# First norm of a two-block transformer kernel: every squared chunk summed on TensorE, the first phase table moved ahead of it on VectorE, block positions transferred before the input

## The chip, the core and the metric

One core of a Trainium2 chip runs the whole program. Its engines are TensorE (PE, with its weight loads shown as PEld), VectorE (DVE), ScalarE (ACT), GpSimd (POOL) and SyncE (SP), which here only issues transfers. Each runs its own stream of instructions in order, and they wait for each other by semaphores. The metric is the device time of one execution in microseconds (us).

## The reference

Input `x` is 512 tokens of width 1024, fp32. A first block (norm, a projection that feeds an S5 state-space branch and stick-breaking attention, gates, a feed-forward part) is followed by a second block of two layers (gated linear attention, forgetting attention, each with a per-layer embedding). What matters here is the first norm and what stands right behind it:

```python
def rmsnorm(x, g):
    xf = x.astype(jnp.float32)
    y = xf * lax.rsqrt(jnp.mean(xf * xf, axis=-1, keepdims=True) + EPS)
    return (y * g.astype(jnp.float32)).astype(x.dtype)
...
        u = rmsnorm(h, norm_mix[l])
        proj = u @ w_in[l]
        u_ssm, q, k, v = jnp.split(proj, [D_SSM, D_SSM + D_ATTN, D_SSM + 2 * D_ATTN], axis=-1)
```

The S5 branch needs, for each state, powers of `exp(lam * dt)` at the positions of the blocks of 4 tokens. Their angle is the "phase": block position times turns per token, less the whole turns.

## The kernel before

**Layout.** `h` holds the input feature-major: 8 chunks (DC) of 128 features on the partitions, 512 tokens along the free dimension. The fp32 products are made as three products of fp32r halves (`three`, L526 to L533: high by high, high by low, low by high), so each operand is split into a high and a low part: ScalarE makes the high part by a rounding copy (L1222), VectorE the low part by a subtraction.

**Weights.** 105 units of 1 MB (`wstream`) go through two slots `wraw`. SyncE issues the first two at the start (L433) and each further one when the low part of the unit before in the slot is done (L444 to L449). ScalarE splits high (`split_hi`, L1224), VectorE low (`split_lo`, L1908).

**Transfers at the start**, all on SyncE's queue, in this order (L423 to L442): the S5 parameters, `ones`, the input in four parts (`x_in`), `vecs`, `ident`, two weight units, the S5 coefficient matrices `s5b` (semaphore `bc_in`), then `headones`, `samechunk`, `reset` and `blockpos`, five constants to be rounded, and `wa2`. These last ten count on `cst_sem` (N_CST is 10).

**The first norm.** ScalarE squares the chunks (L1829 to L1831) into `first_square(c)`. VectorE's `first_norm` (L1983) adds chunks 0 to 6 into `acc`. TensorE sums over the partitions: a product whose stationary operand is 128 tokens of a squared chunk and whose moving operand is one column of ones. `first_sums` (L586) does that for the last chunk, then for `acc`, four products each, into four columns of a PSUM bank. VectorE then computes the reciprocal root by shift and three Newton steps (`norm_rms`, `rsqrt`, L1926 to L1950), TensorE spreads it over the partitions (`norm_spread`, L617), and VectorE scales each chunk (L2011), ScalarE rounds it, VectorE makes its low part (L2001), and the first projection unit (`gemm(0, ...)`) takes chunk by chunk.

**Unread products.** `unread(n)` (L581) issues n 128x512 fp32 products of a tile of zeros into a bank that nobody reads. The order on TensorE is written out by hand:

```python
            pe.wait_ge(x_in[1], 16)
            unread(3)
            pe.wait_ge(first_in, 48)
            first_sums()
            unread(2)
            norm_spread(0)
            unread(3)
            gemm(0, 0, two(0), 256, uhi, ulo, True, u_wait(0), ready=0)
```

**The phase and what follows.** On VectorE `s5_prepare` (L2032) makes the turns per token and per the low part. Behind `first_norm`, the second weight unit's low part and four small vector steps stands `phase(0)` (L2102): seven steps over 128x512, each waiting for the one before. ScalarE's `table(0)` (L1325) makes sine and cosine of it. Then VectorE builds the input maps (`in_maps(0)`, L2070), the low parts of queries and keys, and enters the loop of four mixers, in which the order on VectorE is `out_maps`, `softplus`, `fail_lo`, `turn_in` (with the repeated map, L2152), `w_lo` and so on. `phase(i + 1)` for the later mixers is made inside mixer i.

Of the kernel before, what the change touches and what calls it, by code (L numbers as in the profile page):

```python
# [21 lines left out]
ALU = mybir.AluOpType  # L22
# [3 lines left out]
P = 128  # L26
T = 512
D = 1024
DC = D // P
TT = T // P  # L30
# [51 lines left out]
CST = {}  # L82
# [39 lines left out]
def build(nc, wstream, xT, pT, vecs_d, cst_d, s5p_d, wa2_d, outT):  # L122
    ctx = ExitStack()
    with ctx:
# [3 lines left out]
        def sem(name):  # L128
            return ctx.enter_context(nc.semaphore(name))
# [12 lines left out]
        ones = sb("ones", [P, P])  # L142
        headones = sb("headones", [P, P])
# [162 lines left out]
        N_CST = 10  # L306
# [22 lines left out]

        x_in = [sem(f"x_in{k}") for k in range(X_PARTS)]  # L330
        first_in, cst_sem, par_in, pe_sem = sem("vectors_in"), sem("consts_in"), sem("params_in"), sem("ple_in")
        bc_in = sem("bc_matrices_in")
        out_sem = sem("out_stored")
        landed = [sem("weights_landed0"), sem("weights_landed1")]
        hi_done, lo_done = sem("weights_hi_done"), sem("weights_lo_done")
# [67 lines left out]
        def first_square(c):  # L403

            return pp[:, c, :] if c < DC - 2 else sq[:, c % 2, :]
# [15 lines left out]
        @block.sync  # L421
        def _(sp):
            sp.dma_start(s5p[:, 0:3, :], s5p_d[:, 0:48].rearrange("p (a b) -> p a b", a=3)).then_inc(par_in, 16)  # L423
            a, b = CST["ones"]
            sp.dma_start(ones[:, :], cst_d[:, a:b]).then_inc(first_in, 16)
            for k in range(X_PARTS):
                c = slice(k * DC // X_PARTS, (k + 1) * DC // X_PARTS)
                sp.dma_start(h[:, c, :], xT[:, c, :]).then_inc(x_in[k], 16)
            sp.dma_start(vecs[:, :], vecs_d).then_inc(first_in, 16)
            a, b = CST["ident"]  # L430
            sp.dma_start(ident[:, :], cst_d[:, a:b]).then_inc(first_in, 16)
            for n in range(2):
                sp.dma_start(wraw[:, n, :], wstream[n]).then_inc(landed[n], 16)  # L433
            sp.dma_start(s5b[:, :, :], s5p_d[:, 48:].rearrange("p (a b) -> p a b", a=4)).then_inc(bc_in, 16)
            for name, dst in (("headones", headones), ("samechunk", samechunk), ("reset", reset),
                              ("blockpos", blockpos)):
                a, b = CST[name]
                sp.dma_start(dst[:, :], cst_d[:, a:b]).then_inc(cst_sem, 16)
            for k, name in enumerate(("ones", "keymask", "querymask", "tri", "negones")):
                a, b = CST[name]  # L440
                sp.dma_start(cst_in[:, k, :], cst_d[:, a:b]).then_inc(cst_sem, 16)
            sp.dma_start(wa2[:, :], wa2_d).then_inc(cst_sem, 16)  # L442

            with nc.sync.Fori(0, (NU - 3) // 2) as i:  # L444
                for n in range(2):
                    sp.wait_ge(lo_done, i * 2 + (n + 1))
                    sp.dma_start(wraw[:, n, :], wstream[i * 2 + (n + 2)]).then_inc(landed[n], 16)
            sp.wait_ge(lo_done, NU - 2)
            sp.dma_start(wraw[:, 0, :], wstream[NU - 1]).then_inc(landed[0], 16)  # L449
            for k in range(TT // 2):  # L450
                for half in range(2):
                    for t, evacuated in ((2 * k, out_even), (2 * k + 1, out_odd)):
                        sp.wait_ge(evacuated, 2 * k + half + 1)
                        sp.dma_start(outT[:, t, half * T:half * T + T], h[:, 2 * t + half, :]).then_inc(out_sem, 16)
            sp.wait_ge(out_sem, 16 * DC)
# [69 lines left out]
        def _(pe):  # L525
# [55 lines left out]
            def unread(n):  # L581

                for _ in range(n):
                    nc.tensor.matmul(ps[:, 0, :], M[:, 0, :], M[:, :, :].rearrange("p q c -> p (q c)"), start=True, stop=True)

            def first_sums():  # L586

                pe.wait_ge(sq_done, DC)
                for t in range(TT):
                    nc.tensor.matmul(ps[:, SS_BANK[0], t:t + 1], first_square(DC - 1)[:, t * P:(t + 1) * P], ones[:, 0:1],  # L590
                                     start=t == 0, stop=False, skip_group_check=True)
                pe.wait_ge(acc_done, DC - 1)
                for t in range(TT):
                    mm = nc.tensor.matmul(ps[:, SS_BANK[0], t:t + 1], acc[:, t * P:(t + 1) * P], ones[:, 0:1], start=False,
                                          stop=True, skip_group_check=True)
                mm.then_inc(ss_done, 1)

            def norm_sums(j):

# [17 lines left out]
            def norm_spread(j, k=0, bank=None):  # L617

                pe.wait_ge(rs_done, j + 1)
                for t in range(TT):  # L620
                    mm = nc.tensor.matmul(ps[:, SS_BANK[j] if bank is None else bank, t * P:(t + 1) * P],  # L621
                                          rstd[:, k, t:t + 1].to_broadcast([P, P]), ident[:, :], start=True, stop=True)
                mm.then_inc(bc_done, 1)
# [533 lines left out]

            pe.wait_ge(bias_ready, 1)
            pe.wait_ge(x_in[1], 16)
            unread(3)  # L1160
            pe.wait_ge(first_in, 48)
            first_sums()
            unread(2)
            norm_spread(0)
            unread(3)
            gemm(0, 0, two(0), 256, uhi, ulo, True, u_wait(0), ready=0)
# [50 lines left out]
        def _(act):  # L1217
# [619 lines left out]
                other = HEAD_ROWS[1 - hh]  # L1837
                own.do(copy(kl[other, hh, :], zero_b[other, :].to_broadcast([64, T])))
            norm(0)
            act.wait_ge(bc_in, 16)  # L1840
            own.do(copy(s5b[:, 3, :], s5b[:, 3, :], -1.0))
            act.wait_ge(cst_sem, 16 * N_CST)
            for k, dst in enumerate((onesr, keymaskr, querymaskr, trir, negonesr)):
                copy(dst[:, :], cst_in[:, k, :]).then_inc(consts_ready, 1)
            copy(identr[:, :], ident[:, :]).then_inc(consts_ready, 1)
# [58 lines left out]
        def _(dve):  # L1904
# [77 lines left out]

            def first_norm():  # L1983

                for c in range(1, DC - 1):
                    dve.wait_ge(sq_done, c + 1)
                    if c >= 2:
                        dve.wait_ge(acc_done, c - 1)
                    V.tensor_tensor(acc[:, :], first_square(0) if c == 1 else acc[:, :], first_square(c),
                                    ALU.add).then_inc(acc_done, 1 if c < DC - 2 else 2)  # L1990
                dve.wait_ge(first_in, 48)
                norm_rms(0)

                def weights_lo(half):
                    at = slice(UW // 2 * half, UW // 2 * half + UW // 2)
                    dve.wait_ge(hi_done, 1)
                    return V.tensor_tensor(wlo[:, 0, at], wraw[:, 0, at], whi[:, 0, at], ALU.subtract)

                def lo(c):
                    dve.wait_ge(u_hi, c + 1)  # L2000
                    V.tensor_tensor(ulo[:, c, :], un[:, c % 2, :], uhi[:, c, :], ALU.subtract).then_inc(u_ready, 1)  # L2001

                own.do(weights_lo(0))
                dve.wait_ge(bc_done, 1)
                for c in range(DC):
                    if c >= 2:
                        lo(c - 2)
                        dve.wait_ge(u_ready, c - 1)
                    if c == DC // 2 + 1:
                        weights_lo(1).then_inc(lo_done, 1)  # L2010
                    V.scalar_tensor_tensor(un[:, c % 2, :], h[:, c, :], vec("norm_mix", c), ps[:, SS_BANK[0], :], ALU.mult,  # L2011
                                           ALU.mult).then_inc(un_done, 1)
                lo(DC - 2)
                lo(DC - 1)
# [55 lines left out]
            def in_maps(i):  # L2070

                if i == 0:
                    dve.wait_ge(bc_in, 16)
                    dve.wait_ge(powers_ready, 2 * L)
                else:
                    dve.wait_ge(in_tr, i)
                part = tmp[:, :, 0:L, :]
                own.do(V.tensor_tensor(ET[:, 0, :, :, :], matrix(i, 0, L), powers(i, 1, 0, L), ALU.mult))
                own.do(V.tensor_tensor(part, matrix(i, 1, L), powers(i, 1, 1, L), ALU.mult))
                own.sync()  # L2080
                step(V.tensor_tensor(ET[:, 0, :, :, :], ET[:, 0, :, :, :], part, ALU.subtract))
                own.do(V.tensor_tensor(ET[:, 1, :, :, :], matrix(i, 0, L), powers(i, 1, 1, L), ALU.mult))
                own.do(V.tensor_tensor(part, matrix(i, 1, L), powers(i, 1, 0, L), ALU.mult))
                own.sync()
                V.tensor_tensor(ET[:, 1, :, :, :], ET[:, 1, :, :, :], part, ALU.add).then_inc(in_gen, 1)
# [594 lines left out]


            s5_prepare()
            first_norm()
            split_static(1)
            own.do(V.tensor_tensor(g12[:, :], vecs[:, VEC["norm_final"]:VEC["norm_final"] + DC],
# [2 lines left out]
            own.do(V.memset(gs[:, :, 0], 1.0))  # L2688
            own.do(V.tensor_tensor(gs[:, :, 1], gain, gain, ALU.mult))
            own.do(V.tensor_scalar(negb[:, :], vecs[:, VEC["gla_b_a"]:VEC["gla_b_a"] + GLA_H], -1.0, None, ALU.mult))  # L2690
            dve.wait_ge(cst_sem, 16 * N_CST)
            phase(0)
            in_maps(0)
            q_lo(0)
            k_lo(0)
# [224 lines left out]
```

## Time and profile before

| what | value |
|---|---|
| runs | 1411.25, 1411.37, 1412.5 us; median 1411.37 |
| the profiled execution: its own time | 1411.53 us |
| its span in the trace | 1409.7 us |
| TensorE busy | 1378.5 us |
| VectorE busy | 954.5 us |
| ScalarE busy | 736.8 us |
| GpSimd busy | 61.3 us |
| mean granted clock of TensorE | 0.997 |

The own time contains 1.8 us around the span. Times in the trace count from the span's start. Products are pipelined: the duration of one is longer than the distance to the next, so the pace is read from the starts. An fp32 product leaves two records of a weight load and two of a product.

### The profile page before, as it was taken

The page shows a single profiled execution, that of the slowest core. Times are in us where ns is not written, and L with a number is a line of the kernel's source. Part 1 is how long each engine was busy: PE and PEld are TensorE (multiplying, and loading weights), DVE is VectorE, ACT ScalarE, POOL GpSimd, SP SyncE. Part 2 cuts the span into 40 slices and gives each one's busy share as a digit, 9 for nine tenths or more (in the row PEclk, how much of TensorE's full clock was granted, in tenths as well). Part 3 has the DMA queues.
Part 4 walks back from the last instruction along what each step waited for, and adds up shares of the span by engine and source line. Part 5 has one row for each costly group of instructions (what it writes and reads, how often), then busy time and mean ns, then how long its engine had stood idle before and what let it go on. Part 6 is the DMA issues. An engine that isn't in the chain of part 4 may idle for free.

```text
span 1409.7 us, 18398 instructions
## 1 busy us (share of the span) xinstructions
PE 1378.5 (98%) x7012; PEld 1164.7 (83%) x7012; DVE 954.5 (68%) x1328; ACT 736.8 (52%) x1043; POOL 61.3 (4%) x74
## 2 busy tenths in 40 slices
PE   7999999999999999999999999999999999999997
PEld 4888888788888888888889999888878888887876
DVE  7999985425554444444455877665879999998574
ACT  6777776232332222223246444434568888888353
POOL 2000000000200000000000000011100000000311
PEclk9999999999999999999999999999999999999998
DMA  6111103222313223222322111222221221211311
GB/s 216 56 60 60 61 1 116 94 90 90 113 68 118 90 91 117 82 98 90 111 84 100 65 60 60 105 96 84 90 90 60 78 71 60 89 60 43 122 60 60
DMA packets 19307, 118.37 MB, mean 84 GB/s; under 512 B 2401, under 2 KB 3681, under 8 KB 5681
## 3 DMA queue, kind: packets, MB, share of 16 engines
q1 hardware_dynamic: 18960, 116.51, 23.4%
q0 software_dynamic: 288, 1.05, 0.2%
q8 instruction: 41, 0.67, 0.2%
q14 instruction: 18, 0.14, 0.0%
HBM read 115.45 MB, written 2.10 MB: 83 GB/s over the span
## 4 chain that ended last, share of the span: by engine, by line
PE 81%; DVE 5%; ACT 2%; issue 1%; DVEq 0%
PE ps L528 25%; PE ps L530 24%; PE ps L529 24%; PE ps L1052 1%; DVE wlo L1910 1%; PE ps L1085 1%; PE ps L1042 1%; PE ps L1083 1%; PE ps L1044 1%; PE ps L610 0%; PE ps L621 0%; PE ps L1011 0%; PE ps L1046 0%; ACT whi L1222 0%; PE ps L950 0%
## 5 line engine op out<-in xcount | busy, mean ns | idle before, releaser
L528 PE MATMUL ps<-uhi,whi 128*128 128x512 f32 x1060 | 420.5, 397 | 4.0 <-DVE ulo L2474 1.6
L530 PE MATMUL ps<-uhi,wlo 128*128 128x512 f32 x1060 | 413.5, 390 | 0.0
L529 PE MATMUL ps<-ulo,whi 128*128 128x512 f32 x1060 | 412.9, 389 | 0.0
L1910 DVE TENSOR_TENSOR wlo<-wraw,whi 128x2048 fp32r<-128x2048 f32 x104 | 241.3, 2321 | 107.1 <-ACT whi L1222 106.1
L1222 ACT ACTIVATE whi<-wraw 128x2048 fp32r<-128x2048 f32 x105 | 200.5, 1909 | 170.9 <-PE ps L530 169.0
L528 PEld LDWEIGHTS ps<-uhi,whi 128*128 128x128 f32 x1060 | 199.2, 188 | 47.7 <-DVE wlo L1910 2.3
L530 PEld LDWEIGHTS ps<-uhi,wlo 128*128 128x128 f32 x1060 | 198.9, 188 | 42.7
L529 PEld LDWEIGHTS ps<-ulo,whi 128*128 128x128 f32 x1060 | 199.3, 188 | 38.3
L528 PE MATMUL ps<-hdhi,whi 128*128 128x512 f32 x256 | 99.6, 389 | 0.0
L529 PE MATMUL ps<-hdlo,whi 128*128 128x512 f32 x256 | 99.6, 389 | 0.0
L530 PE MATMUL ps<-hdhi,wlo 128*128 128x512 f32 x256 | 99.6, 389 | 0.0
L1497 ACT ACTIVATE hd<-rl 128x512 f32<-128x512 f32 x32 | 20.2, 632 | 115.6 <-DVE rl L2297 115.6
L2306 DVE TENSOR_TENSOR h<-ps,h 128x512 f32<-128x512 f32 x64 | 43.7, 690 | 44.1 <-PE ps L530 44.1
L2297 DVE SCALAR_TENSOR_TENSOR rl<-ps,rms_ff 128x512 f32<-128x512 f32 x32 | 22.0, 690 | 70.3 <-PE ps L530 70.2
L528 PEld LDWEIGHTS ps<-hdhi,whi 128*128 128x128 f32 x256 | 48.0, 188 | 10.1
L529 PEld LDWEIGHTS ps<-hdlo,whi 128*128 128x128 f32 x256 | 48.0, 188 | 10.0
L530 PEld LDWEIGHTS ps<-hdhi,wlo 128*128 128x128 f32 x256 | 48.0, 188 | 9.9
L412 POOL TENSOR_TENSOR acc<-acc,sq 128x512 f32<-128x512 f32 x25 | 41.0, 1640 | 83.0 <-ACT sq L1240 82.0
L2302 DVE TENSOR_TENSOR hdlo<-hd,hdhi 128x512 fp32r<-128x512 f32 x32 | 20.7, 689 | 33.9 <-ACT hdhi L1222 33.9
L2276 DVE TENSOR_TENSOR h<-ps,h 128x512 f32<-128x512 f32 x24 | 16.4, 689 | 37.3 <-PE ps L530 37.3
L1240 ACT ACTIVATE sq<-h 128x512 f32<-128x512 f32 x40 | 24.1, 621 | 30.3 <-DVE h L2276 21.3
L1743 ACT ACTIVATE pr<-ps,nmax 128x512 f32<-128x512 f32 (+1 forms) x64 | 32.8, 524 | 10.6 <-DVE nmax L2582 10.6
(481 smaller groups left out, 2518.3 us busy)
## 6 DMA issues: line engine op xcount, KB each, us to landing
wraw<-wstream SPq DMA_DIRECT2D x105, 1024.0 KB, 4.8
h<-xT SPq DMA_DIRECT2D x4, 512.0 KB, 5.7
outT<-h SPq DMA_DIRECT2D x8, 256.0 KB, 2.9
s5b<-s5p_d SPq DMA_DIRECT2D x1, 1024.0 KB, 12.1
pe_in<-pT POOLq DMA_DIRECT2D x2, 512.0 KB, 4.5
cst_in<-cst_d SPq DMA_DIRECT2D x5, 64.0 KB, 10.0
reset<-cst_d SPq DMA_DIRECT2D x1, 256.0 KB, 11.0
wa<-wa_d SPq DMA_DIRECT2D x1, 160.0 KB, 5.9
```

Source lines behind the costliest of these rows:

```text
L412: eng.tensor_tensor(acc[:, :], sq[:, 0, :] if c == 1 else acc[:, :], sq[:, c % 2, :], ALU.add).then_inc(acc_done, 1)
L528: nc.tensor.matmul(out, lh, rh, start=start, stop=False, skip_group_check=True)
L529: nc.tensor.matmul(out, lh, rl_, start=False, stop=False, skip_group_check=True)
L530: mm = nc.tensor.matmul(out, ll, rh, start=False, stop=stop, skip_group_check=True)
L1222: return A(out, in_, ACT.Copy, scale=scale)
L1240: A(both_square(c) if j == BOTH else sq[:, c % 2, :], h[:, c, :], ACT.Square).then_inc(sq_done, 1)
L1497: A(hd[:, m % 2, :], rl[:, m % 2, :], ACT.Square).then_inc(hd_done, 1)
L1743: e = A(pr[:, at], zf[:, at], ACT.Exp, bias=nmax[:, col], accum_out=rsum[:, col])
L1910: V.tensor_tensor(wlo[:, slot, :], wraw[:, slot, :], whi[:, slot, :], ALU.subtract).then_inc(lo_done, 1)
L2297: V.scalar_tensor_tensor(rl[:, m % 2, :], ps[:, a + m, :], 0.0, rms_ff[:, :], ALU.max, ALU.mult).then_inc(rl_done, 1)
L2302: V.tensor_tensor(hdlo[:, m, :], hd[:, m % 2, :], hdhi[:, m, :], ALU.subtract).then_inc(hd_ready, 1)
L2306: V.tensor_tensor(h[:, m, :], ps[:, bank, :], h[:, m, :], ALU.add).then_inc(h_added, 1)
```

## The change

TensorE: `first_sums` is replaced by `first_chunk_sums(c)`, called for each of the eight chunks, with four one-column products each, all accumulating in the same four columns. Two unread products come before, one after every second chunk, and four more after the last; before, there were three ahead of the sums and two behind. The semaphore `acc_done` gets its whole count from TensorE at chunk 6. VectorE: the six additions are gone; `phase(0)` stands between `s5_prepare` and the first norm. SyncE: `blockpos` is transferred right behind `ones`, ahead of the input, and both count on a new semaphore; `s5b` joins the constants' semaphore, whose total stays ten, and the waits for `bc_in` become waits for all ten.

```diff
-            a, b = CST["ones"]
-            sp.dma_start(ones[:, :], cst_d[:, a:b]).then_inc(first_in, 16)
+            for name, dst in (("ones", ones), ("blockpos", blockpos)):
+                a, b = CST[name]
+                sp.dma_start(dst[:, :], cst_d[:, a:b]).then_inc(early_in, 16)
...
-            sp.dma_start(s5b[:, :, :], s5p_d[:, 48:].rearrange("p (a b) -> p a b", a=4)).then_inc(bc_in, 16)
-            for name, dst in (("headones", headones), ("samechunk", samechunk), ("reset", reset),
-                              ("blockpos", blockpos)):
+            sp.dma_start(s5b[:, :, :], s5p_d[:, 48:].rearrange("p (a b) -> p a b", a=4)).then_inc(cst_sem, 16)
+            for name, dst in (("headones", headones), ("samechunk", samechunk), ("reset", reset)):
...
-            def first_sums():
-
-                pe.wait_ge(sq_done, DC)
-                for t in range(TT):
-                    nc.tensor.matmul(ps[:, SS_BANK[0], t:t + 1], first_square(DC - 1)[:, t * P:(t + 1) * P], ones[:, 0:1],
-                                     start=t == 0, stop=False, skip_group_check=True)
-                pe.wait_ge(acc_done, DC - 1)
-                for t in range(TT):
-                    mm = nc.tensor.matmul(ps[:, SS_BANK[0], t:t + 1], acc[:, t * P:(t + 1) * P], ones[:, 0:1], start=False,
-                                          stop=True, skip_group_check=True)
-                mm.then_inc(ss_done, 1)
+            def first_chunk_sums(c):
+
+                pe.wait_ge(sq_done, c + 1)
+                for t in range(TT):
+                    mm = nc.tensor.matmul(ps[:, SS_BANK[0], t:t + 1], first_square(c)[:, t * P:(t + 1) * P], ones[:, 0:1],
+                                          start=c == 0 and t == 0, stop=c == DC - 1, skip_group_check=True)
+                if c == DC - 2:
+                    mm.then_inc(acc_done, DC - 1)
+                if c == DC - 1:
+                    mm.then_inc(ss_done, 1)
...
             pe.wait_ge(x_in[1], 16)
-            unread(3)
-            pe.wait_ge(first_in, 48)
-            first_sums()
             unread(2)
+            pe.wait_ge(early_in, 32)
+            for c in range(DC):
+                first_chunk_sums(c)
+                if c % 2:
+                    unread(1)
+            unread(4)
+            pe.wait_ge(first_in, 32)
             norm_spread(0)
...
             norm(0)
-            act.wait_ge(bc_in, 16)
+            act.wait_ge(cst_sem, 16 * N_CST)
             own.do(copy(s5b[:, 3, :], s5b[:, 3, :], -1.0))
-            act.wait_ge(cst_sem, 16 * N_CST)
...
             def first_norm():
 
-                for c in range(1, DC - 1):
-                    dve.wait_ge(sq_done, c + 1)
-                    if c >= 2:
-                        dve.wait_ge(acc_done, c - 1)
-                    V.tensor_tensor(acc[:, :], first_square(0) if c == 1 else acc[:, :], first_square(c),
-                                    ALU.add).then_inc(acc_done, 1 if c < DC - 2 else 2)
-                dve.wait_ge(first_in, 48)
                 norm_rms(0)
...
                 if i == 0:
-                    dve.wait_ge(bc_in, 16)
+                    dve.wait_ge(cst_sem, 16 * N_CST)
                     dve.wait_ge(powers_ready, 2 * L)
...
             s5_prepare()
+            dve.wait_ge(early_in, 32)
+            phase(0)
+            dve.wait_ge(first_in, 32)
             first_norm()
...
-            dve.wait_ge(cst_sem, 16 * N_CST)
-            phase(0)
             in_maps(0)
```

## Rows read from the trace of the kernel before

**Rows 1.** The profile page: busy time of each engine, and the chain that ended last, by engine.
```profile
PE 1378.5 (98%) x7012; PEld 1164.7 (83%) x7012; DVE 954.5 (68%) x1328; ACT 736.8 (52%) x1043; POOL 61.3 (4%) x74
...
PE 81%; DVE 5%; ACT 2%; issue 1%; DVEq 0%
```
**Rows 2.** Timeline of the lead, all engines: start us, us, engine, line, what, count [idle before].
```profile
6.30 0.17 DVE L2060 TENSOR_TENSOR s5p<-s5p 128x16 f32<-128x16 f32 x1
...
7.39 5.17 PE L584 MATMUL ps<-M 128*128 128x512 f32 x6 [7.39 <-DMA h<-xT]
...
10.17 1.15 ACT L1831 ACTIVATE sq<-h 128x512 f32<-128x512 f32 x2 [0.16 <-DMA h<-xT]
...
11.20 0.69 DVE L1989 TENSOR_TENSOR acc<-acc,sq 128x512 f32<-128x512 f32 x1
...
12.39 0.95 PE L590 MATMUL ps<-ones,sq 128*128 128x1 f32 x8
...
13.20 1.03 PE L594 MATMUL ps<-ones,acc 128*128 128x1 f32 x8
...
14.10 1.96 PE L584 MATMUL ps<-M 128*128 128x512 f32 x4
...
14.35 0.16 DVE L1942 TENSOR_SCALAR rs_half<-ps 128x4 f32<-128x4 f32 x1 [2.46 <-PE ps L594]
...
16.99 0.31 DVE L1920 SCALAR_TENSOR_TENSOR rstd<-rs_t,rs_y 128x4 f32<-128x4 f32 x1
...
17.36 1.16 PE L621 MATMUL ps<-ident,rstd 128*128 128x128 f32 x8 [1.30 <-DVE rstd L1920]
...
18.35 2.74 PE L584 MATMUL ps<-M 128*128 128x512 f32 x6
...
20.77 0.56 PE L528 MATMUL ps<-uhi,whi 128*128 128x512 f32 x1
```
**Rows 3.** Line L584, the unread products: duration ns min/median/max, first and last start us.
```profile
L584 PE MATMUL ps<-M x16: 592/594/1193, 7.4 to 20.5; 128*128 128x512 f32 x16
```
**Rows 4.** Timeline of PE further on, sums between products.
```profile
741.01 0.95 PE L610 MATMUL ps<-gs,pp 128*128 128x2 f32 x8
741.82 0.49 PE L528 MATMUL ps<-uhi,whi 128*128 128x512 f32 x1
```
**Rows 5.** Timeline of the issues on SyncE's queue.
```profile
1.68 1.85 SPq L428 DMA_DIRECT2D h<-xT  x4
...
15.01 0.44 SPq L442 DMA_DIRECT2D wa<-wa_d  x1
```
**Rows 6.** Windows view: busy PE, PEld, DVE, ACT, POOL; PEclk; DMA share; GB/s.
```profile
6.00:9.00 3.00, 1.61 (x2) 0.84 (x3) 2.01 (x6) 2.44 (x5) 0.00 (x0) 1.00 1.00 385
```
**Rows 7.** Timeline of DVE behind the lead.
```profile
33.30 0.69 DVE L2107 TENSOR_TENSOR rin<-blockpos,s5p 128x512 f32<-128x512 f32 x1
...
37.13 0.69 DVE L2113 TENSOR_TENSOR cosT<-rin 128x512 f32<-128x512 f32 x1
...
53.02 1.49 DVE L2189 SCALAR_TENSOR_TENSOR att<-ps,att 128x1280 f32<-128x1280 f32 x1
...
59.52 0.69 DVE L2152 COPY Es<-ET 128x1024 f32<-128x1024 f32 x1
...
61.66 1.49 DVE L2197 TENSOR_TENSOR atlo<-att,athi 128x1280 fp32r<-128x1280 f32 x1 [0.25 <-ACT athi L1222]
```
**Rows 8.** Timeline of PE behind the lead: its two waits.
```profile
55.87 0.50 PE L732 MATMUL ps<-athi,trir 128*128 128x512 f32 x1 [0.30 <-ACT athi L1222]
...
60.35 2.02 PE L680 MATMUL ps<-H,Es 128*128 128x128 f32 x16 [1.37 <-DVE Es L2152]
```
**Rows 9.** Timeline of ACT in the same stretch.
```profile
50.47 1.37 ACT L1365 ACTIVATE att<-att,biases 128x1280 f32<-128x1280 f32 x1
...
59.02 1.24 ACT L1375 ACTIVATE att<-ps 128x1280 f32<-128x1280 f32 x1 [1.40 <-PE ps L732]
```
**Rows 10.** The windows view at the program's end; PEclk is the granted clock.
```profile
1400.00:1411.00 11.00, 0.94 (x6) 0.56 (x5) 3.21 (x7) 3.04 (x7) 0.00 (x0) 0.56 0.51 191
```

More of the change, by code:

```diff
@@ L331, in build @@
         first_in, cst_sem, par_in, pe_sem = sem("vectors_in"), sem("consts_in"), sem("params_in"), sem("ple_in")
-        bc_in = sem("bc_matrices_in")
+        early_in = sem("ones_and_block_positions_in")
         out_sem = sem("out_stored")
```

## The prediction

> **What bounds the kernel now.** I read the page first. TensorE (PE) is busy 98% of the span and the chain that ended last lies on it for 81%, with nearly nothing of the rest in waits [rows 1]. A microsecond by which PE's stream of products starts later is therefore a microsecond on the end, and one that VectorE (DVE) gives back counts only where PE waits for it. So the case is decided by two stretches: the lead, up to the first product of the projection, and the first places behind it where PE waits for something that the moved VectorE work made late.
>
> The timeline of the lead [rows 2] shows the order. PE starts at 7.39, when the second part of the input has landed, with the three unread products (six records, since each fp32 product is two passes). Meanwhile ScalarE squares the chunks, the last pair from 10.17 to 11.32, and VectorE adds six of them, the last until 11.89. PE comes to its sums only at 12.39: a group of eight records for the last chunk, one of eight for the accumulated rest from 13.20, and at 14.10 it is past them. VectorE begins the root at 14.35, has it at 17.30, and the spread starts at 17.36; PE, through its two unread products by 16.06, waited 1.30 us for it. From the spread on everything hangs in one line: scale, split high, split low, first product at 20.77. So the lead is set by the sums on PE and then by the root on VectorE, not by the additions.
>
> **The part on PE.** The sources and the timeline give the two prices. An unread product's record takes 1193 ns at first and 592 to 594 ns later [rows 3]: TensorE's lower level (1.2 GHz) and its upper (2.4). The granted clock reads 1.00 from 6 to 9 already [rows 6], so at the start the records decide, not that column. At the upper level six records from 18.35 take 2.74 us [rows 2], so one follows the other after (2.74 − 0.59) / 5 = 0.43 us and an unread product costs 0.86 us, at the lower level twice that, 1.71. A group of eight sum records costs 0.81 us at the upper level: 741.01 to 741.82, in the same form of loop further on, with products on either side [rows 4], and 12.39 to 13.20 here. What moves is one column or two; the price is in the eight weight loads.
>
> How the level rises: six records at 0.855 would have let PE go on at 7.39 + 5.13 = 12.52; it went on at 12.39, so the rise fell shortly before, about 12.15, 4.75 us after PE's first instruction.
>
> After the change PE has ahead of the root: 2 unread products, 8 groups of sums in place of 2, and 3 unread products between them. Behind the last group stand 1 + 4 unread products in place of 2. Worked out:
> - Start. One more transfer of 64 KB is issued ahead of the input. Four input issues take 1.85 us, 0.46 each [rows 5], so the input can be 0.46 later at most; if the transfer were swallowed, 0. Its bytes at the 385 GB/s of 6 to 9 us are 0.17 [rows 6]. I take 0.3, between the two: PE starts at 7.69. VectorE's wait for it costs nothing, as its preparation ends at 6.47 [rows 2]; with that cover gone the phase would begin later in VectorE's idle time, still at no cost.
> - 2 unread products at the lower level, 3.42: 11.11.
> - The rise at 7.69 + 4.75 = 12.44. Until then 1.33 us do what 0.67 us do at the upper level. What is left is 8 × 0.81 + 3 × 0.86 = 9.06 less 0.67, so 8.39: PE is past the sums at 20.83. The squares are long there (the last at 11.6), no group waits.
> - Before it was 14.10: the sums end **6.7 us later**.
> - The root follows 0.25 after PE is past the sums and takes 2.95 (14.35 to 17.30), so it is there at 24.0. PE is still in its five unread products, 4.28 us, until 25.1, and only then comes to the spread: 1.1 more. The spread starts at 25.1 against 17.36, **+7.7 us**.
>
> The six more groups and the five more unread products (10 ahead of the spread in place of 5) are work that nothing else needs; they lie wholly ahead of the spread. VectorE's six additions (to 11.89) are removed at no gain, since PE did not come to its sums before 12.39.
>
> **The part on VectorE.** The phase is seven instructions, 33.30 to 37.82 less the overlap, 4.4 us in line [rows 7], ahead of the input maps. It goes into 6.5 to 10.9, where VectorE only added. Everything behind it on VectorE can come 4.4 earlier relative to the spread, but what of it reaches PE is small. PE is full from 33.21 to 55.57; then it waits 0.30 for ScalarE and 1.37 for VectorE's repeated map [rows 8]: 1.67 us together. The VectorE step at 53.02 could move up to the end of ScalarE's logarithm at 51.84 [rows 7, 9], 1.2 at most, so the map at 59.52 and with it PE gain about 1.2. Then VectorE stands behind ScalarE again: its step at 61.66 waits for ScalarE, which itself had waited for PE from the products that gain only the 0.30 [rows 7, 9]. From there on VectorE is 0.3 early, PE 1.2, and the next low parts of the weights catch PE up. Bounds: 0.3 from below, 4.4 from above if VectorE set the pace all along. I take **−0.8**, near the lower ones, as the rows show VectorE behind ScalarE at both places.
>
> The merged semaphores cost nothing: the wait for all constants instead of the coefficient matrices stood already ahead of the maps, and those transfers are issued by 15.45 for a use at 33 [rows 5]; ScalarE's wait at its copies is the same one a step earlier. Without that cover a late constant would hold VectorE's maps.
>
> **Sum.** 1411.53 for the profiled execution (0.16 above the median of the runs), + 7.7 − 0.8 = **1418.4 us**, 0.5% slower.
>
> **The rivals.**
> *The clock stays low through the sums.* In the trace PE had nothing but 512-column products ahead of the rise; after the change two of them are followed by loads with one-column products, a start that the trace doesn't show. At the end of the program, where transposes and such sums stand alone, the granted clock is 0.56 in the last 11 us, partly idle [rows 10]. For: that, and the short first block. Against: between 741 and 755 such groups alternate with products and their price stays 0.81. Price: 9.06 at half speed is 18.1, so the sums end at 29.2, the root at 32.5; five unread products from 29.2, first low, then high after some 4.75 us (2.4 done, 1.9 left), end at 35.9. The spread is 18.5 late, less 0.8: 1429 us. The Trainium skill, "TensorE: Matmul & The Clock Gate", section "What's actually happening", says that "the default state is throttled, and activity releases the throttle"; if loads with one column are no such activity, that is this rival, else the forecast.
>
> *VectorE's 4.4 us counts in full.* Then 1411.53 + 7.7 − 4.4 = 1414.8. For: VectorE is hardly idle from 33 to 61. Against: PE's two waits and the places where ScalarE is the later one [rows 8, 9].
>
> *Faster: the loads run ahead beneath neighbouring products.* The place is the groups of sums, where each group lies beside unread products. With groups at nothing and the rise at 12.44: 5 unread products, 4.28, less 2.38 done before the rise, end at 14.3; the spread is at 18.6, +1.3. With the 4.4 that gives 1408.4; with 0.8 it gives 1412.0, the same. With the 4.4 it decides from a price under (7.7 − 4.4) / 8 = 0.4 below 0.81, so 0.4 us a group. Against: the groups at 741 to 755 have neighbours and cost 0.81.
>
> **How the numbers follow.** A measurement can tell about 0.2%, 2.8 us. Forecast 0.66; clock low 0.20; VectorE in full 0.07; loads hidden 0.07, of it faster 0.03. The forecast's own range: the input between 0 and 0.46 late (−0.3, +0.2), the rise as early as the end of the first block or some 3 us later (−0.7, +1.5), the gain 0.3 to 1.7 (+0.5, −0.9): 1416.6 to 1420.6. To leave out no more than 2 in 10 it reaches up to the low clock: 1416.4 to 1429.0. Slower 0.92 (the first three cases), same 0.05, faster 0.03.
>
> **What would show it.** Right: groups of eight records at 0.81 us eight times, PE never waiting for a square; the start of the root near 21; VectorE idle from 11 to 21; the spread starting the moment the last unread record lets it, near 25, with no wait for the root; the first product near 28.5; the waits at 55.87 and 60.35 smaller and the phase gone from 33. Wrong: records of 1193 ns beyond the first block; a group under 0.5 us; a spread that waits for the root; or, from 34 on, a trace that is over 2 us less behind than at the spread.

## The result, and the profile after

The changed kernel takes 1429.28 us (median of 4 runs, 1427.7 to 1430.18) against 1411.31 for the kernel before: a ratio of 1.0126, 95% interval 1.0114 to 1.0138. The forecast was 1418.4 us, with a range up to 1429.0. The direction held; the size is that of the first rival, the low clock, which was priced at 1429.

The profiled execution (1429.29 us) on its page, as in [rows 1]:

```profile
span 1427.5 us, 18504 instructions
...
PE 1397.9 (98%) x7070; PEld 1180.9 (83%) x7070; DVE 949.6 (67%) x1322; ACT 736.3 (52%) x1043; POOL 59.7 (4%) x74
...
PE 80%; DVE 5%; ACT 2%; issue 1%; DVEq 0%
```

PE is as full as before: it has 19.4 us more of busy time and the end comes 17.8 us later. The timeline of PE in the lead, against [rows 2]:

```profile
7.78 3.75 PE L584 MATMUL ps<-M 128*128 128x512 f32 x4 [7.78 <-DMA h<-xT]
11.32 3.41 PE L590 MATMUL ps<-ones,pp 128*128 128x1 f32 x16
14.59 2.06 PE L584 MATMUL ps<-M 128*128 128x512 f32 x2
16.44 3.41 PE L590 MATMUL ps<-ones,pp 128*128 128x1 f32 x16
...
26.68 3.41 PE L590 MATMUL ps<-ones,sq 128*128 128x1 f32 x16
29.95 6.55 PE L584 MATMUL ps<-M 128*128 128x512 f32 x10
36.34 1.05 PE L620 MATMUL ps<-ident,rstd 128*128 128x128 f32 x8
...
39.62 0.58 PE L528 MATMUL ps<-uhi,whi 128*128 128x512 f32 x1
```

Read the starts, not the durations. Sixteen sum records, which are two groups, last 3.27 us from start to start (11.32 to 14.59) in place of 1.62, and two unread records 1.85 (14.59 to 16.44) in place of 0.86. All four pairs of groups look so, and PE is past the sums at 29.95, not at 20.8. So a group costs 1.64 us instead of 0.81. Of the ten records behind, some are slow and some fast. The forms of line L584 say the same as [rows 3] did, only that now the median too is near the slow level:

```profile
L584 PE MATMUL ps<-M x26: 592/1061/1202, 7.8 to 39.4; 128*128 128x512 f32 x26
```

The trace puts the rise to the upper level at 34.0 us after the span's start; in the kernel before it was at 12.1. The first product is at 39.62 in place of 20.77, 18.85 us later.

VectorE, against [rows 7]:

```profile
6.40 0.69 DVE L2102 TENSOR_TENSOR rin<-blockpos,s5p 128x512 f32<-128x512 f32 x1
...
10.22 0.69 DVE L2108 TENSOR_TENSOR cosT<-rin 128x512 f32<-128x512 f32 x1
30.20 0.16 DVE L1944 TENSOR_SCALAR rs_half<-ps 128x4 f32<-128x4 f32 x1 [19.29 <-PE ps L590]
...
32.38 0.17 DVE L1922 SCALAR_TENSOR_TENSOR rstd<-rs_t,rs_y 128x4 f32<-128x4 f32 x1
...
52.16 0.69 DVE L2073 TENSOR_TENSOR ET<-s5b,s5w 128x512 f32<-128x512 f32 x1
...
70.71 1.49 DVE L2184 SCALAR_TENSOR_TENSOR att<-ps,att 128x1280 f32<-128x1280 f32 x1 [0.20 <-ACT att L1368]
...
77.22 0.68 DVE L2147 COPY Es<-ET 128x1024 f32<-128x1024 f32 x1
...
79.81 1.49 DVE L2192 TENSOR_TENSOR atlo<-att,athi 128x1280 fp32r<-128x1280 f32 x1 [0.71 <-ACT athi L1225]
```

The phase stands where it was meant to, from 6.40 to 10.91, and nothing of it is left in its old place: the input maps stand directly behind the small steps, at 52.16. But from 10.91 to 30.20 VectorE has nothing to do. What it gave back is seen at PE's two waits, against [rows 8]:

```profile
74.17 0.48 PE L731 MATMUL ps<-athi,trir 128*128 128x512 f32 x1
...
78.05 2.02 PE L679 MATMUL ps<-H,Es 128*128 128x128 f32 x16 [0.91 <-DVE Es L2147]
```

The wait of 0.30 is gone and that of 1.37 is 0.91, 0.76 us less in the two together. The step at 60.35 is now at 78.05, 17.70 later where the first product was 18.85 later: 1.15 us given back, and 1.05 by the end of the span (17.8 later). The other 0.39 shows as no wait of its own.

### The profile page after: what moved, and what is told of

Read it like the earlier page. It is cut to its first block, busy times and chain, and to the rows that moved or that the text cites. A ratio compares the mean times of both kernels' runs of the same rounds, so it can differ in the third digit from the quotient of the medians.

```text
span 1427.5 us, 18504 instructions
## 1 busy us (share of the span) xinstructions
PE 1397.9 (98%) x7070; PEld 1180.9 (83%) x7070; DVE 949.6 (67%) x1322; ACT 736.3 (52%) x1043; POOL 59.7 (4%) x74
## 3 DMA queue, kind: packets, MB, share of 16 engines
q0 software_dynamic: 288, 1.05, 0.2%
## 4 chain that ended last, share of the span: by engine, by line
PE 80%; DVE 5%; ACT 2%; issue 1%; DVEq 0%
PE ps L528 25%; PE ps L530 24%; PE ps L529 24%; PE ps L1051 1%; DVE wlo L1912 1%; PE ps L1084 1%; PE ps L1041 1%; PE ps L1082 1%; PE ps L1043 1%; PE ps L609 0%; PE ps L620 0%; PE ps L1010 0%; PE ps L1045 0%; ACT whi L1225 0%; PE ps L949 0%
## 6 DMA issues: line engine op xcount, KB each, us to landing
s5b<-s5p_d SPq DMA_DIRECT2D x1, 1024.0 KB, 11.6
```

## Experiments

The question was whether the clock is the cause, what holds it down, and how much would be left of the loss without it. Theory A: the two products end before the clock's rise, and a third would reach it. Theory B: the groups of one-column sums hold the clock down whatever stands ahead.

**More products ahead of the sums** (e1 three, e2 four).

```diff
-            unread(2)
+            unread(3)      (e1), unread(4)      (e2)
             pe.wait_ge(early_in, 32)
```

> The changed kernel with three unread products ahead of the sums in place of two. Theory A (the two products end before the clock's rise and the groups of sums that follow do not bring it on; one more product reaches over the rise, about 4.75 us after PE's first instruction): rise near 12.5, groups at 0.81 us, sums past at 21.8, spread at 26.0, about 1419 us. Theory B (loads with one-column products keep the clock low whatever stands ahead of them): groups at 1.64 us, one product more at the low level, 1431 us.

> The changed kernel with four unread products ahead of the sums. Theory A: rise near 12.5 as in the run with three, sums past at 22.6, spread at 26.9, about 1420 us, 10 us less than with two although PE has two products more to do. Theory B: the clock falls back or never rises, 1432 us or more. If three are too few and four are enough, the place of the rise varies from run to run.

Measured: 1424.24 us with three (1424.02 to 1429.05) and 1426.37 with four. Theory A wanted 1419 and 1420, theory B 1431 and 1432 or more: both fall as they stood. The windows of the run with three (of its slowest execution, 1429.05; the column after the five engines is the granted clock):

```profile
13.00:16.00 3.00, 3.00 (x24) 2.52 (x22) 0.00 (x0) 2.08 (x2) 2.61 (x12) 1.00 1.00 418
16.10:20.00 3.90, 3.90 (x14) 3.09 (x14) 0.00 (x0) 1.64 (x1) 3.12 (x12) 0.50 1.03 340
20.00:33.00 13.00, 13.00 (x40) 9.19 (x39) 3.10 (x13) 1.25 (x2) 0.00 (x0) 0.50 0.02 6
...
1303.00:1306.00 3.00, 3.00 (x8) 2.33 (x8) 2.62 (x9) 2.40 (x9) 0.00 (x0) 0.50 0.55 232
```

and of the run with four:

```profile
14.00:19.90 5.90, 5.90 (x45) 4.94 (x43) 0.00 (x0) 3.04 (x2) 4.80 (x19) 1.00 1.04 373
20.00:30.00 10.00, 10.00 (x32) 7.36 (x32) 2.47 (x13) 1.25 (x2) 0.00 (x0) 0.50 0.01 3
```

The clock did rise, at 12.6 and 13.1 us, and fell again: at 16.0 in the second pair of groups, at 19.9 in the third. Up to there PE had done pairs of groups with one product behind each, and no idle stretch. The clock came back in the products behind the sums, at 33.1 and 30.2. So in these two executions one product after two groups did not hold it. That is theory C, with which the next runs were made. The other three executions with three products took 1424.0 to 1424.4, at a mean granted clock of 0.994 against 0.990; where they rose and fell no trace shows.

**Two products between, or none** (e7, with four ahead; e3).

```diff
-            unread(2)
+            unread(4)                           (e7 only)
...
                 first_chunk_sums(c)
-                if c % 2:
-                    unread(1)
+                if c % 2:
+                    unread(2)                   (e7; left out in e3)
```

> The changed kernel with four unread products ahead of the sums and two after every second chunk. Theory C in its narrow form (it is the share of one-column groups in the stretch that brings the clock down; with as much time in wide products as in groups it holds): rise near 13, groups at 0.81 us throughout, sums past at 13.9 + 6.5 + 5.1 = 25.5, six products behind in 5.1, spread at 30.7, 1423.7 us, less than the run with one between (1426.4) though it has four products more. In its wide form (any such mixture lets it fall): groups at 1.64 us from 16 to 20 us on, over 1431 us.

> The changed kernel without the unread products between and right behind the groups of sums: two ahead, eight groups in one piece, four behind. Theory C (groups of loads with one-column products bring the clock down or keep it down, and the single unread products between them are too few to matter): groups at 1.64 us, sums past at 11.3 + 13.1 = 24.4, the four behind partly low until about 29.5, spread near 29.7 in place of 36.3: 1422.6 us. Rival (the products between do help the clock, so that without them it is as slow or slower): 1429 us or more.

e7: 1424.65 us. The timeline of PE has every pair of groups in 1.70 us and every two products in 1.80, up to the end of the sums:

```profile
14.68 1.84 PE L590 MATMUL ps<-ones,pp 128*128 128x1 f32 x16
16.38 1.96 PE L584 MATMUL ps<-M 128*128 128x512 f32 x4
18.18 1.84 PE L590 MATMUL ps<-ones,pp 128*128 128x1 f32 x16
...
26.89 5.40 PE L584 MATMUL ps<-M 128*128 128x512 f32 x12
```

The clock held, and the run is 1.7 us faster than e2, which has half as many products between and is otherwise the same. e3: 1422.67 us, 6.6 less than the changed kernel, by leaving four products out:

```profile
11.47 10.23 PE L590 MATMUL ps<-ones,pp 128*128 128x1 f32 x48
21.57 3.55 PE L590 MATMUL ps<-ones,sq 128*128 128x1 f32 x16
24.98 6.45 PE L584 MATMUL ps<-M 128*128 128x512 f32 x8
31.27 1.05 PE L620 MATMUL ps<-ident,rstd 128*128 128x128 f32 x8
```

Eight groups from 11.47 to 24.98 are 1.69 each, low throughout. The single products between bought nothing: with or without them the sums ran at the low level, and without them they ended 5 us sooner. The traced execution took 1424.13 us, 5.2 less than the traced one of the changed kernel; two of the four took 1421.3 and 1421.4 and were not traced.

**The products behind the sums** (e6).

```diff
-                if c % 2:
+                if c % 2 and c < DC - 1:
                     unread(1)
-            unread(4)
```

> The changed kernel without the five unread products behind the last group. Theory: they are 6.4 us on the path at the low clock, of which 2.6 cover the root's time; but they are also what brings the clock up. Without them the spread is at 32.6 in place of 36.3 and runs low (2.07 us in place of 1.05), and the three products behind it run low, to 39.6 at the latest: 1426 to 1429.5 us. Rival (the five are pure delay): 3.8 us less, 1425.5 us or below.

Measured 1426.69 us, 2.6 less than the changed kernel. The spread starts at 32.68 and takes 2.05, at the low level; the rise came at 36.6, in the products behind it:

```profile
32.68 2.05 PE L620 MATMUL ps<-ident,rstd 128*128 128x128 f32 x8 [2.60 <-DVE rstd L1921]
34.52 3.78 PE L584 MATMUL ps<-M 128*128 128x512 f32 x6
37.74 0.79 PE L528 MATMUL ps<-uhi,whi 128*128 128x512 f32 x1
```

So the five products delayed the spread by 3.7 us (36.34 against 32.68), and leaving them out gained 2.6; the rest went where the spread and what follows it ran at the low level.

**What moves in a sum** (e8). The same number of instructions, loads and products in the same order, with 128 moving columns in place of one:

```diff
-                    mm = nc.tensor.matmul(ps[:, SS_BANK[0], t:t + 1], first_square(c)[:, t * P:(t + 1) * P], ones[:, 0:1],
+                    mm = nc.tensor.matmul(ps[:, SS_BANK[0], t * P:(t + 1) * P], first_square(c)[:, t * P:(t + 1) * P], ones[:, :],
...
-                mean = both_sums[:, 0:2 * TT:2] if j == BOTH else ps[:, SS_BANK[j], 0:TT]
+                mean = both_sums[:, 0:2 * TT:2] if j == BOTH else ps[:, SS_BANK[j], 0:TT] if j else ps[:, SS_BANK[0], 0:T:P]
```

> The changed kernel with 128 moving columns of ones in each sum in place of one (the sums then fill a bank, and the root reads every 128th column); as many instructions and weight loads, the same order. Theory D (what keeps the clock down is that one moving column leaves the array idle, not the loads or the number of wide products ahead): the clock rises near 12.5 us and stays, a group costs about 0.9 us (eight records with 128 columns, as in the spread), sums past near 21.5, spread near 25.8, about 1419 us. Rival (the two products ahead are too few whatever follows, or loads as such keep it low): a group 1.7 us or more, 1430 us.

```profile
11.34 2.10 PE L590 MATMUL ps<-ones,pp 128*128 128x128 f32 x16
...
19.42 1.95 PE L590 MATMUL ps<-ones,sq 128*128 128x128 f32 x16
21.20 4.46 PE L584 MATMUL ps<-M 128*128 128x512 f32 x10
25.50 1.05 PE L620 MATMUL ps<-ident,rstd 128*128 128x128 f32 x8
...
28.79 0.57 PE L528 MATMUL ps<-uhi,whi 128*128 128x512 f32 x1
```

1418.59 us, 10.7 us less than the changed kernel by giving PE more to multiply. The rise is at 11.6 us, right behind the two products, the groups cost 0.89 and PE is past the sums at 21.20. This run settles the question: with the same loads, the same products ahead and between and the same order, the clock rose at 11.6 with 128 moving columns and at 34.0 with one. So neither the number of loads nor the two products ahead are the reason here. Widths between 1 and 128 were not run. Of the 18.0 us that the change lost, at least 10.7 are thus the clock's (the wide groups cost a little more themselves); the other 7.3 are what the change costs without it.

**The leanest form tried** (e9): e8 without the products between and with two behind.

```diff
                 first_chunk_sums(c)
-                if c % 2:
-                    unread(1)
-            unread(4)
+            unread(2)
```

> As the run with 128 moving columns, without the unread products between the groups and with two behind them in place of five. Theory D: clock high from about 12.5 us, sums past at 19.0, root at 22.2, spread at 22.3, 4.9 later than in the kernel before, less 1.0 given back: 1415.3 us. That would be the floor of summing every chunk on TensorE in this order. Rival: the clock stays low, sums past at 25.6 us, over 1421 us.

```profile
11.28 6.16 PE L590 MATMUL ps<-ones,pp 128*128 128x128 f32 x48
17.28 1.95 PE L590 MATMUL ps<-ones,sq 128*128 128x128 f32 x16
19.07 1.88 PE L584 MATMUL ps<-M 128*128 128x512 f32 x4
21.82 1.13 PE L620 MATMUL ps<-ident,rstd 128*128 128x128 f32 x8 [0.88 <-DVE rstd L1920]
```

1414.83 us, ratio to the kernel before 1.0026 (1.0015 to 1.0037). The clock rose at 12.6 us and stayed. Even so eight groups on PE are past at 19.07, where two groups and VectorE's additions were past at 14.10 [rows 2].

**The two halves of the change** (e4: the phase back in its old place; e5: the kernel before with the phase ahead of the additions, and with the changed kernel's transfers and waits for them, which are not shown below).

```diff
e4           dve.wait_ge(early_in, 32)
-            phase(0)
...
+            phase(0)
             in_maps(0)
e5           s5_prepare()
+            dve.wait_ge(early_in, 32)
+            phase(0)
             first_norm()
```

> The changed kernel with the phase back in its old place behind the norm on VectorE; TensorE's part and the transfers as changed. Theory: the phase's move gives back about 1.05 us (the lead is 18.85 later at the first product, the end 17.8), so this is 1430.3 us. Rival (VectorE's 4.4 us count in full and something else is slower by as much): 1433.7 us.

> The kernel before with the phase ahead of the additions on VectorE and block positions transferred ahead of the input; sums as before (six additions on VectorE, two groups on TensorE). The additions run from 10.9 to 15.2 in place of 7.2 to 11.9, the root starts near 16.4, 2.05 later, the give-back is 1.05: 1412.3 us. Rival (VectorE's 4.4 us count in full): 1409 us.

e4: 1429.04 us median, not to be told from the changed kernel, as its four executions spread over 2.9 us and those of the changed kernel over 2.5. Its trace tells more:

```profile
39.82 0.57 PE L528 MATMUL ps<-uhi,whi 128*128 128x512 f32 x1
...
74.90 0.50 PE L731 MATMUL ps<-athi,trir 128*128 128x512 f32 x1 [0.33 <-ACT athi L1225]
...
79.38 2.02 PE L679 MATMUL ps<-H,Es 128*128 128x128 f32 x16 [1.36 <-DVE Es L2147]
```

The first product is 0.20 later than in the changed kernel, the step at 79.38 is 1.33 later: the waits of [rows 8] are back in full (0.33 and 1.36). The phase's move is worth 1.1 us at that place, not 4.4. This rests on one trace of each; the medians, 0.24 apart the other way, cannot tell it.

e5: 1413.86 us (1.0016, 1.0006 to 1.0025), 1.6 over what was expected. Its profiled execution:

```profile
13.46 1.37 PE L590 MATMUL ps<-ones,sq 128*128 128x1 f32 x8
15.54 1.05 PE L594 MATMUL ps<-ones,acc 128*128 128x1 f32 x8 [0.71 <-DVE acc L1989]
...
19.61 2.07 PE L621 MATMUL ps<-ident,rstd 128*128 128x128 f32 x8 [0.67 <-DVE rstd L1920]
```

Sums and root were about as late as expected (the last group from 15.54, the root from 16.70), but the clock, up at 14.3, was low again from 17.8 to 24.6, and the spread took 2.07. It fell while PE was in its two unread products, behind a wait of 0.71 us and before that of 0.67. The kernel before has the same groups and products and a wait of 1.30 behind them, and its clock stayed; what made the difference is not shown.

**Other ways to the same end** (b1: three of the phase's steps in VectorE's wait for the sums; b2: the last chunk added by VectorE, one group on PE, two steps in the wait). Both are the kernel before, with block positions transferred behind the identity matrix and the remaining steps of the phase in the old place, which is not shown below.

```diff
b1, b2           dve.wait_ge(first_in, 64)
+                phase(0, range(3))                  (b2: range(2))
                 norm_rms(0)
b2
-                for c in range(1, DC - 1):
+                for c in range(1, DC):
...
-                pe.wait_ge(sq_done, DC)
-                for t in range(TT):
-                    nc.tensor.matmul(ps[:, SS_BANK[0], t:t + 1], first_square(DC - 1)[:, t * P:(t + 1) * P], ones[:, 0:1],
-                                     start=t == 0, stop=False, skip_group_check=True)
                 pe.wait_ge(acc_done, DC - 1)
```

> The kernel before with the first three of the phase's seven steps in the 2.46 us in which VectorE waits for the sums (block positions transferred behind the identity matrix, so the input is not later); TensorE's order as before. Theory: the sums and the spread stay where they were (14.1, 17.36), VectorE is 1.9 us ahead behind the norm, which covers all that TensorE waited for, as the whole phase did in the changed kernel: 1.05 less than the kernel before, 1410.1 us. Rival (what it gives back is lost again further on, as VectorE's second low parts of weights set the pace): no change.

> The kernel before turned the other way: VectorE adds the last chunk too, TensorE has one group of sums in place of two, and the first two of the phase's seven steps stand in VectorE's wait. Theory: last addition to 12.6, group 12.65 to 13.46, root started at 13.8 in place of 14.35, spread at 16.8: 0.55 earlier, and what VectorE gives back is 0.8 or so: 1409.8 us. Rival (TensorE's work behind the norm is held by other waits): within 0.2% of the kernel before, as with three steps moved.

b1: 1410.73 us, ratio 0.9995 (0.9985 to 1.0004). b2: 1410.15 us, 0.9992 (0.9983 to 1.0001). Neither can be told from the kernel before, though both are on the right side. b2's lead:

```profile
12.82 1.35 PE L591 MATMUL ps<-ones,acc 128*128 128x1 f32 x8
14.04 1.96 PE L585 MATMUL ps<-M 128*128 128x512 f32 x4
16.82 1.16 PE L618 MATMUL ps<-ident,rstd 128*128 128x128 f32 x8 [0.82 <-DVE rstd L1917]
```

The group started at 12.82 as planned but took 1.22 us to the next start, as the clock rose only at 13.5 in this execution (12.1 in that of the kernel before); the spread came 0.54 sooner. All 11 runs of b2 lie within 0.8 us, where those of the kernel before spread over 2.3.

## Why the prediction was wrong

- **The start.** PE began at 7.78, 0.39 late; 0.3 was taken, between bounds of 0 and 0.46. Right for this execution; the other runs with the same transfers began between 7.73 (e2) and 8.21 (e5).
- **The prices.** Near enough. At the upper level e7 shows 0.85 us a group and 0.90 an unread product (1.70 and 1.80 for two), where 0.81 and 0.86 were taken; the changed kernel shows 1.64 and 1.85 at the lower level.
- **The rise at 12.44.** This step failed. It carried the 4.75 us after PE's first instruction over from an execution in which PE had done nothing but 512-column products, to one in which it turned to one-column sums after 3.5 us. The rise came at 34.0, after 4.1 us of the products behind the sums, so a group cost 1.64 us in place of 0.81 and PE was past the sums at 29.95 in place of 20.83. With 128 moving columns the rise came at 11.6, and the kernel took 1418.59. That this is the forecast's number to 0.2 us is partly luck: the wide groups cost 0.08 more each, 0.6 in all, the rise was 0.8 early, and 0.2 more was given back. The 4.75 itself came from one execution. Where the clock rose ahead of the sums or early in them, it did so 3.8 (e8) to 6.2 us (e7) after PE's first instruction.
- **The argument against the rival.** It held up the groups at 741 to 755, where the clock stayed [rows 4]. Each of those has three 512-column products of 0.79 us together behind it (741.82 to 742.61), about as much time as the group, and so it is in e7, where the clock held. In the changed kernel one product of 0.86 stands to two groups of 1.62 at the upper level, and e1 and e2 show the clock falling in that. The rows were right and were taken for another mixture. The other sign, the end of the program [rows 10], was misread: PE is busy for 0.94 of those 11 us, so its 0.56 is mostly idle time. Just ahead, from 1395 to 1400 us, transposes and such sums ran back to back and the granted clock was 1.00. That the rival came true owes nothing to this row. The Trainium skill ("TensorE: Matmul & The Clock Gate", "What's actually happening") says that activity releases the throttle. The traces do not contradict it, but it does not decide this case: PE was busy without a gap from 7.8 us on both in e8 and in the changed kernel, and the clock rose at 11.6 in one and at 34.0 in the other.
- **The order behind the sums.** Root found before the unread products ended, spread directly behind them: right at both clocks (root at 32.5, spread at 36.3; the rival's text had 32.5 and 35.9). The root's time agrees by two errors: the sums ended 0.75 later than the rival's 29.2, and the root took 2.35 us (30.20 to 32.55) and not 2.95.
- **The give-back.** 0.8 taken, 1.05 to 1.15 measured, inside the bounds; the 4.4 in full is refuted by e4. The thought that ScalarE is the later one at 53 and 61 us holds: the same steps wait for it at 70.71 and 79.81.
- **Loads hidden beneath neighbours.** Refuted: between unread products the groups cost 0.85 us in e7 and 1.64 in the changed kernel.
- **The range** ended at 1429.0, at the rival's central value and not at its upper edge; the changed kernel's own four executions lie between 1427.7 and 1430.18.

What stays open is how the moments of rise and fall are set. Executions of the same kernel lie up to 5 us apart (e1, whose slowest also has the late fall told below), and no run here was made to tell why.

## What to carry to other kernels

Before work is moved to TensorE, price it in weight loads and ask at which clock it will run: sums with one moving column cost nearly the same as with 128 at the upper level (0.81 to 0.85 against 0.89 us a group), and in e1 and e2 the clock fell while they had little else between them. Idle filler is worth its time only where the granted clock in the trace shows that it holds the level; here the products between the groups, one to two groups, cost 5 us and held nothing. And an operation moved on an engine that is not the bottleneck gained here about what PE had been waiting for it, 1.1 us of 4.4, not its own length.

## What was not expected

- More work made it faster: 128 moving columns in place of one took 10.7 us off (e8), and four unread products more made e7 1.7 us faster than e2. The prediction had no place for this; the texts of these two runs did.
- The clock fell for a while late in the program too: in e1 the granted clock was 0.50 from 1302.9 to 1306.3 (above), in b1's profiled execution from 1285.5 to 1288.9. Both falls come within about 1 us of a wait of PE for VectorE, 1.56 us up to 1302.51 and 1.58 up to 1284.48. The kernel before has the same wait, 1.60 up to 1285.84, and no fall behind it, so the wait alone is not the reason. In b1 the fall cost 1.2 us: PE was 1.34 us ahead of the kernel before in front of it (1281.08 against 1282.42) and 0.13 behind it (1291.28 against 1291.41). That is most of why b1's trace is 1.46 us ahead at the step of 60.35 and only 0.4 at the end.
- In the windows view the granted clock reads 1.00 before its first change, although the records there are twice as long; the column can be trusted only from the first rise on. The same goes for the mean over an execution. The changed kernel's fastest execution (1427.7) has a mean of 0.990, the other three 0.996 to 0.997; in e3 and e4 too the two faster executions have the lower mean (0.991 to 0.993 against 0.997 to 0.998). An early rise with a fall behind it, as in e1, would give just that, but none of these faster executions was traced.
